# A transformer pair on one Trainium2 core: the closing norm takes the root with half of its squares as the bias, and the work tiles begin 128 bytes lower

## What is computed

```python
def rms_norm(x, g):
    xf = x.astype(jnp.float32)
    y = xf * lax.rsqrt(jnp.mean(xf * xf, axis=-1, keepdims=True) + EPS)
    return (y * g.astype(jnp.float32)).astype(x.dtype)
...
        h = rms_norm(x, norm_ffn_pre[l])
        f = (jax.nn.silu(h @ w_gate[l]) * (h @ w_up[l])) @ w_down[l]
        x = x + rms_norm(f, norm_ffn_post[l])
```

## Time and profile before

| | |
|---|---|
| median of 3 runs | 2140.75 us |
| lowest and highest | 2138.17 and 2142.24 us |
| the profiled execution | 2137.94 us |
| its span, first to last instruction | 2136.0 us |
| PE busy | 2018.4 us, 94% |
| POOL busy | 1456.1 us, 68% |
| DVE busy | 966.7 us, 45% |
| ACT busy | 514.0 us, 24% |
| mean granted clock of TensorE | 0.980 |

### The profile page before, as it was taken

One profiled execution on the slowest core, in us unless ns is written; L12 is line 12 of the kernel. 1 busy time (PEld: TensorE's weight loads), 2 busy tenths in 40 slices (PEclk: granted clock), 3 DMA queues, 4 the chain that ended last, 5 costly groups with the idle time before them and its releaser, 6 DMA issues.

```text
span 2136.0 us, 25931 instructions
## 1 busy us (share of the span) xinstructions
PE 2018.4 (94%) x8925; PEld 1615.1 (76%) x8925; DVE 966.7 (45%) x1187; ACT 514.0 (24%) x935; POOL 1456.1 (68%) x1668
## 2 busy tenths in 40 slices
PE   7999999999999999789999999999998879999998
PEld 5888888777777877767788888876677648888886
DVE  6423230588655477656432221037776484233101
ACT  3111100343444432430211110022555432111001
POOL 5777776777755656448777777676564567777766
PEclk9999999999999999999999999999999889999999
DMA  5233332322212223002333332233010013333322
GB/s 170 85 94 94 93 98 89 86 83 80 60 41 59 62 67 89 21 20 89 89 90 97 98 89 99 90 87 89 20 30 21 20 40 88 90 98 89 108 94 74
DMA packets 256183, 164.46 MB, mean 77 GB/s; under 512 B 30204, under 2 KB 245310, under 8 KB 255982
## 3 DMA queue, kind: packets, MB, share of 16 engines
q1 hardware_dynamic: 254304, 157.90, 25.2%
q10 hardware_dynamic: 1806, 5.58, 0.7%
HBM read 161.33 MB, written 2.13 MB: 77 GB/s over the span
## 4 chain that ended last, share of the span: by engine, by line
PE 78%; DVE 10%; POOL 6%; issue 3%; ACT 2%; ACTq 1%; DMA 0%; DVEq 0%; POOLq 0%
PE bank L820 12%; PE bank L821 12%; PE bank L822 12%; PE bank L1098 4%; PE bank L1100 4%; PE bank L1099 4%; PE bank L916 4%; PE bank L918 4%; PE bank L917 4%; POOL w_lo L674 3%; PE bank L911 2%; PE bank L913 2%; PE bank L912 2%; PE bank L994 2%; DVE work L2355 1%
## 5 line engine op out<-in xcount | busy, mean ns | idle before, releaser
L674 POOL TENSOR_TENSOR w_lo<-raw,w_hi 128x256 fp32r<-128x256 f32 x1192 | 952.7, 829 | 24.9
L670 POOL TENSOR_SCALAR w_hi<-raw 128x1024 fp32r<-128x1024 f32 x298 | 321.7, 1079 | 452.2 <-PE bank L822 187.3
L820 PE MATMUL bank<-u_hi,w_hi 128*128 128x512 f32 x1056 | 422.6, 400 | 16.6 <-DVE u_lo L2209 15.5
L821 PE MATMUL bank<-u_lo,w_hi 128*128 128x512 f32 x1056 | 419.2, 397 | 0.0
L822 PE MATMUL bank<-u_hi,w_lo 128*128 128x512 f32 x1056 | 419.0, 397 | 0.0
L820 PEld LDWEIGHTS bank<-u_hi,w_hi 128*128 128x128 f32 x1056 | 200.2, 190 | 70.1 <-issue 18.0
L822 PEld LDWEIGHTS bank<-u_hi,w_lo 128*128 128x128 f32 x1056 | 200.5, 190 | 47.0
L821 PEld LDWEIGHTS bank<-u_lo,w_hi 128*128 128x128 f32 x1056 | 200.7, 190 | 46.6 <-issue 0.7
L1098 PE MATMUL bank<-u_hi,w_hi 128*128 128x512 f32 x464 | 194.6, 419 | 2.5 <-POOL w_lo L674 1.4
L1100 PE MATMUL bank<-u_hi,w_lo 128*128 128x512 f32 x464 | 184.1, 397 | 0.0
L1099 PE MATMUL bank<-u_lo,w_hi 128*128 128x512 f32 x464 | 183.6, 396 | 0.0
(11 more groups left out here) (514 smaller groups left out, 3464.7 us busy)
## 6 DMA issues: line engine op xcount, KB each, us to landing
raw<-in_w_in SPq DMA_DIRECT2D x52, 512.0 KB, 3.7
raw<-in_ffn_w_gate SPq DMA_DIRECT2D x44, 512.0 KB, 3.7
raw<-in_ffn_w_up SPq DMA_DIRECT2D x44, 512.0 KB, 3.8
raw<-in_ffn_w_down SPq DMA_DIRECT2D x44, 512.0 KB, 3.3
raw<-in_w_gate SPq DMA_DIRECT2D x22, 512.0 KB, 3.7
raw<-in_w_up SPq DMA_DIRECT2D x22, 512.0 KB, 3.8
raw<-in_w_down SPq DMA_DIRECT2D x22, 512.0 KB, 3.2
raw<-in_w_branch SPq DMA_DIRECT2D x12, 512.0 KB, 3.4
```

The source lines that it names most:

```text
L670: pool.tensor_scalar(w_hi[:, s, :], raw[:, k, :], 1.0, 1.0, ALU.mult, ALU.mult).then_inc(hi_done, 1)
L674: pool.tensor_tensor(w_lo[:, s, c], raw[:, k, c], w_hi[:, s, c].bitcast(F32), ALU.subtract).then_inc(low_quarter if quarter < 3 else split ...
L820: pe.matmul(outs[:, 0:n], wh, rhs_hi[:, c, :], start=(c == 0), stop=False)
L821: pe.matmul(outs[:, 0:n], wh, rhs_lo[:, c, :], start=False, stop=False)
```

## The change

The three small tiles of the last norm are taken out of the row of placed tiles and put at a fixed address behind the largest use of the region (`f_total` is now called `f_part`). What was placed behind them, `work` and the whole region, thereby begins 128 bytes lower.

In the last norm DVE no longer adds the two sums. It makes f_part = sum of the first half / D + EPS, from the first square alone, and ACT takes the root of (sum of the second half) / D + f_part, with f_part as its bias. ACT's root of token tile i stands directly behind the second square of this tile; before it stood one square later.

```diff
-        f_sums, f_total, f_root = (place(n, [P, 8]) for n in ("f_sums", "f_total", "f_root"))
         root_one = place("root_one", [P, 8])
...
-        assert b2a + 10 * 2048 <= nc.sbuf_usable_end
+        assert b2a + 10 * 2048 <= s_at + 49152
+        f_at = s_at + 49152
+        f_sums, f_part, f_root = (at(n, [P, 8], f_at + 32 * k) for k, n in enumerate(("f_sums", "f_part", "f_root")))
+        assert f_at + 96 <= nc.sbuf_usable_end
...
             def token_std(i):
+                act.wait_ge(t_sq, 2 * i + 2)
                 act.wait_ge(t_add, i + 1)
-                act.activation(f_root[:, i:i + 1], f_total[:, i:i + 1], ACT.Sqrt, scale=1.0 / D, bias=EPS).then_inc(t_std, 1)
+                act.activation(f_root[:, i:i + 1], f_sums[:, 2 * i + 1:2 * i + 2], ACT.Sqrt, scale=1.0 / D,
+                               bias=f_part[:, i:i + 1]).then_inc(t_std, 1)
             for b in range(2 * TT):
                 token_square(b)
-                if b >= 2 and b % 2 == 0:
-                    token_std(b // 2 - 1)
-            token_std(TT - 1)
+                if b % 2:
+                    token_std(b // 2)
...
+            def token_part(i):
+                dve.wait_ge(t_sq, 2 * i + 1)
+                dve.tensor_scalar(f_part[:, i:i + 1], f_sums[:, 2 * i:2 * i + 1], 1.0 / D, EPS,
+                                  ALU.mult, ALU.add).then_inc(t_add, 1)
+
             def token_rows(i):
-                dve.wait_ge(t_sq, 2 * i + 2)
-                dve.tensor_tensor(f_total[:, i:i + 1], f_sums[:, 2 * i:2 * i + 1], f_sums[:, 2 * i + 1:2 * i + 2],
-                                  ALU.add).then_inc(t_add, 1)
                 dve.wait_ge(t_std, i + 1)
...
             for i in range(TT):
+                token_part(i)
                 token_rows(i)
```

## The result

The changed kernel takes 2105.51 us (median of 4 runs, 2104.64 to 2106.17) beside 2141.49 us for the kernel before (4 runs, 2138.17 to 2142.88): a ratio of 0.9834, 95% interval 0.9817 to 0.9851. That is 36 us faster. The forecast was 2140.2 us in a range from 2137.1 to 2142.6: it was wrong. Of its own list, the case that came true is rival 4, given 0.09 and sized at 4.6 us.

What follows compares the result with a forecast made beforehand. PE's matmuls, busy 94% of the span, were taken as the bound. Token tile 0 -0.5, tiles 1 to 3 0, addresses 0: -0.5 us from the median 2140.75 gives 2140.2 us, range 2137.1 to 2142.6.

Steps and rivals of the forecast that it cites:

- rival 4: Matmuls: the relation of the operands' residues modulo 256 was bad and becomes good, 1 ns a matmul, 2135.6 us; chance 0.09.
- The addresses: Everything from work on starts 128 bytes lower; matmuls and transfers cost the same at either residue modulo 256: zero.
- Rivals 3 and 4: Matmuls: changed relation of operand residues, 1 ns each, slower (2144.8 us, chance 0.08) or faster (2135.6 us, chance 0.09).
- x_tok and the stores: Load of x_tok and the last stores, from addresses 128 bytes lower: cost zero.
- the bound of 0.4: Load of x_tok, 2048 KB: at most 0.4 us either way, four times the 0.1 us between two 512 KB loads.
- Token tile 0: Last norm: the first root stands directly behind the second square and starts 0.50 to 0.58 us earlier; 0.5 taken.
- Tokens 1 to 3: Last norm, later token tiles: f_part is held by POOL as f_total was, same period of 2.59 us, gain nothing.
- I take 0.79: Last norm: f_part assumed to take 0.79 us, held by POOL's additions, rather than 0.16 unheld.
- Rival 1: Last norm: f_part is not held, tiles 1 to 3 save 0.63 each until POOL binds; -1.1 us, 2139.6 us; chance 0.22.
- ACT's order: Last norm: fifth and sixth squares now stand behind tile 1's root, covered by 1.1 us of slack: cost zero.
- no change: Whole kernel: measured time within 0.2% (4.3 us) of the kernel before; chance 0.83.

Runs made afterwards that it cites:

- addr_only: The kernel before with only the three small tiles moved, so work begins 128 bytes lower, and the last norm kept: 2106.65 us, ratio 0.985.
- root_only: The changed kernel with 128 bytes of padding that put work back to 77312, so only the last norm is changed: 2139.15 us, ratio 1.0.

## Why the prediction was wrong, point by point

*The addresses ("Cost zero").* This step failed, and with it the forecast. It compared L820, which streams a tile from behind work, with L911, which streams one from before it, found 393 and 394 ns, and took that as proof that the residue costs nothing. But both lines have one operand on either side of work, so both had the bad distance of 128: the two rows were two samples of the same slow case. The time lay in the relation, -4.9 ns on 7241 intervals, and what was put at zero was -33 us of the kernel's time (`addr_only`), with -36.9 in these intervals. Rows at the good distance were in the trace of before, but not among the lines that were compared: in the attentions of the second block both operands lie behind work. Timeline of PE in the kernel before:

```profile
1492.88 0.39 PE L1038 MATMUL bank<-b_ph,a_vh 128*128 128x512 f32 x1
1493.10 0.39 PE L1039 MATMUL bank<-prob_lo,a_vh 128*128 128x512 f32 x1
1493.33 0.39 PE L1040 MATMUL bank<-b_ph,a_vl 128*128 128x512 f32 x1
1493.56 0.39 PE L1009 MATMUL bank<-q2h,a_k1h 128*128 128x512 f32 x1
1493.78 0.39 PE L1013 MATMUL bank<-q2l,a_k1h 128*128 128x512 f32 x1
```

By the unrounded starts these are 227, 226, 227 and 227 ns apart. Where streaming tile, weights in use and weights loaded next all lie behind work, 55 of 233 intervals from 215 to 260 ns are 226 or 227 in the kernel before; of the 6506 between matmuls of a weight tile and a tile behind work, 4 are.

*Rivals 3 and 4.* They named the right mechanism, the relation of the two residues, and gave it 0.17 for both directions. Three things were off. The size: 1 ns a matmul was picked, about the price at which it would begin to be seen, and not read from a row; the measured one is 4.9. The count: 4560 matmuls of six lines, where 7241 intervals are in the average and all matmuls with weights from w_hi or w_lo are of this kind. And the words "nothing in the trace hints that their relation would": the intervals did. They ran 228, 230, 233, 241 in a stage where PE waited for nobody, and the shortest of the cycle, 228, hints at what the matmul can do with. 232.4 - 228 = 4.4 ns on 7247 intervals is 32 us, an estimate for rival 4 that the trace of before held, as did the 227 of the attentions. It should also have set the low end of the range, at about 2108.

*x_tok and the stores.* "Cost zero" did not hold here either, but the bound of 0.4 did. From issue to landing the load of x_tok takes 7.56 us before and 7.90 after. Over all runs, with one trace each, it takes 7.53 to 7.61 us in the four kernels in which x_tok begins on a multiple of 256 and 7.64 to 8.05 in the ten in which it does not, on average 0.27 us more; the first matmul starts at 9.5 us before and at 10.0 after. By the Trainium skill, "DMA: Bandwidth & Descriptors", section "How a descriptor splits into AXI transactions", it would be an estimated 0.23 us. The landings agree with that in size. The median packet of 4 KB took 159 ns on and off the boundary, so the packets do not show where the time goes. The stores took a median of 2.0 us in both kernels.

*Token tile 0.* Forecast 0.50 to 0.58 us earlier; measured 1.99 - 1.42 = 0.57. The root itself, though, took 294 ns in place of 194 to 203, now with its bias read from a tile; that was not in the sum.

*Tokens 1 to 3.* "I take 0.79" was wrong: f_part took 141 to 155 ns all four times. The durations by line of the changed kernel:

```profile
L2965 DVE TENSOR_SCALAR f_part<-f_sums x4: 141/144/155, 2091.0 to 2097.7; 128x1 f32<-128x1 f32 x4
...
L2192 ACT ACTIVATE f_root<-f_sums,f_part x4: 294/294/297, 2091.6 to 2097.9; 128x1 f32<-128x1 f32 x4
...
L796 POOL TENSOR_TENSOR out_tok<-out_tok,h_tok x6: 1269/1275/1289, 2093.0 to 2099.1; 128x512 f32<-128x512 f32 x6
```

Rival 1 was right in its mechanism. Three f_part ran beside POOL's additions without being held, where L2337 with four elements had been. A token tile saved 0.50 us and not the 0.63 that rival 1 had, since DVE now waits 0.42 us for the root where it waited 0.27. POOL became the bound: its last addition ran until 2100.4, and the first of DVE's two last additions, which began at 2099.74 beside it, took 1223 ns where the second took 678:

```profile
L2980 DVE TENSOR_TENSOR out_tok<-out_tok,h_tok x2: 678/950/1223, 2099.7 to 2100.9; 128x512 f32<-128x512 f32 x2
```

Rival 1 gave -1.1 us, the trace -1.3. The step that failed is the one from L2337 to f_part: L2337 has four elements, takes a maximum and reads one scalar from a tile (sink); f_part has one element, multiplies and adds, and has two constants. Which of these differences frees it from POOL no run here shows.

*ACT's order.* Covered, as said: the roots of tiles 1 to 3 waited for f_part alone, 0.64 or 0.65 us each, and never for a square.

*The chances.* 0.83 on "no change" rested on where the diff's instructions are. A change of addresses has no instructions, and reaches every one.

## What to carry to other kernels

Where a padding or a small tile shifts large tiles, the operands of every matmul move against each other, so price it by all matmuls and not by the tiles moved. In a stage where PE waits for nobody, take the intervals between starts: if they vary in a fixed cycle above a floor, the matmuls may be held by something that no wait shows, and the mean less the floor, times the count, is an estimate of what there is to win (32 us here, where the intervals gave 36.9). Then try the tile bases of stationary and streaming operands at one residue modulo 256; here it is worth 1.6% of the kernel for no work, and any new `place` between the two groups of tiles can lose it again unless their bases are kept at one residue.

## What the runs showed of the hardware that was not expected

- Float32r matmuls of 512 columns with a weight load each start every 227 ns in the gate, up and last down projections (226 or 227, at the clock's higher level of 2.4 GHz, granted at 1.00 in that stretch) when both tiles' addresses agree modulo 256. At the other distances tried (+32, +64, 128, -64, -32) the mean over a kernel is 229.6 to 233.0 ns, in cycles of a few unequal intervals.
- The cost is not symmetric: 64 bytes one way costs 2 ns (229.2 and 228.9) and the other way 6 (233.3 and 233.3), and which way is which depends on the tile that streams.
- A TENSOR_SCALAR on one element per partition with two constants was not held by POOL (141 to 145 ns for the three that ran beside its additions, and again in `root_only`), one on four elements with a scalar from a tile was (423 ns). The Trainium skill, "SBUF — State Buffer", section "Who interferes with whom", says which DVE instructions can take the port pair that they share with GpSimd; the four-element row agrees with it, and the one-element rows are a case in which a tensor_scalar was not held.
- A load of 2 MB in rows of 4 KB landed on average 0.27 us later when its tile began off a multiple of 256 bytes (7.53 to 7.61 us in four runs on it, 7.64 to 8.05 in ten off it).
